# Two attention stages: weighted sums and later scores in one visit, both heads' products alternating, softmax steps half a step later

## The reference

```python
def fox_attention(q, k, v, log_f):
    ...
        s = jnp.einsum('bqhd,bkhd->bhqk', qi.astype(jnp.float32), kf) * scale
        s = s + ci[..., None] - c[:, :, None, :]
        ...
        p = jax.nn.softmax(s, axis=-1).astype(v.dtype)
        return jnp.einsum('bhqk,bkhd->bqhd', p, v)

def second_block(x, norm_g, fox_w_in, fox_b_f, fox_w_out, swa_w_in, swa_sinks, swa_w_out, final_g):
    ...
            y = fox_attention(q, k, v, log_f)          # layer 0; layer 1: swa_attention(q, k, v, sinks)
    ...
        y = y * jax.nn.silu(gate)
        x = x + y @ w_out
    return rmsnorm_2(x, final_g)
```

## Time and profile before

| | |
|---|---|
| time, median of 3 runs | 2133.93 us (2133.89 to 2136.4) |
| the profiled execution: its time | 2136.29 us |
| its span, first to last instruction | 2134.5 us |
| TensorE busy (its clock 0.999 of full speed) | 2119.7 us, 99% |
| VectorE busy | 1615.8 us, 76% |
| ScalarE busy | 1325.8 us, 62% |
| all the ACT_TABLE_LOADs | 24.4 us in 19 of them |

### The profile page before, as it was taken

One profiled execution on the slowest core, in us unless ns is written; L12 is line 12 of the kernel. 1 busy time (PEld: TensorE's weight loads), 2 busy tenths in 40 slices (PEclk: granted clock), 3 DMA queues, 4 the chain that ended last, 5 costly groups with the idle time before them and its releaser, 6 DMA issues.

```text
span 2134.5 us, 34503 instructions
## 1 busy us (share of the span) xinstructions
PE 2119.7 (99%) x13406; PEld 1852.0 (87%) x13406; DVE 1615.8 (76%) x2945; ACT 1325.8 (62%) x2601; POOL 9.7 (0%) x22
## 2 busy tenths in 40 slices
PE   9999999999999999999999999999999999999998
PEld 8888888888898888888888888888888888988887
DVE  7898766787688888656888867777686777698774
ACT  6866446775576666544666666555556655567764
POOL 0000000000000000000000000000000000000000
PEclk9999999999999999999999999999999999999999
DMA  7544434565465555555555555555555565554464
GB/s 273 168 152 135 153 112 146 188 239 195 158 196 190 193 193 196 197 191 194 195 192 195 190 196 188 206 170 195 183 181 176 166 200 192 193 163 151 148 207 138
DMA packets 107619, 389.31 MB, mean 182 GB/s; under 512 B 12304, under 2 KB 12560, under 8 KB 106688
## 3 DMA queue, kind: packets, MB, share of 16 engines
q1 hardware_dynamic: 105264, 377.31, 53.1%
q0 software_dynamic: 1904, 9.47, 1.2%
q10 hardware_dynamic: 288, 0.32, 0.0%
HBM read 384.34 MB, written 2.13 MB: 181 GB/s over the span
## 4 chain that ended last, share of the span: by engine, by line
PE 92%; DVE 4%; ACT 2%; issue 1%; DMA 0%; SPq 0%; DVEq 0%; ACTq 0%
PE main L564 85%; PE two L564 5%; DVE W L1041 1%; PE two L567 1%; DVE gt L1041 1%; ACT L1708 0%; DVE GK L1047 0%; ACT W L1709 0%; DMA RAW<-ws 0%; ACT NT L1709 0%; DVE PB L1041 0%; DVE GV L1047 0%; DVE GQ L1047 0%; PE main L611 0%; ACT PP L1709 0%
## 5 line engine op out<-in xcount | busy, mean ns | idle before, releaser
L1709 ACT ACTIVATE W<-RAW 128x512 fp32r<-128x512 f32 x1416 | 881.1, 629 | 623.8 <-PE main L564 620.5
L564 PE MATMUL main<-A,W 128*128 128x256 f32 (+1 forms) x7264 | 1256.2, 333 | 3.0 <-DVE W L1041 3.0
L1041 DVE TENSOR_TENSOR W<-RAW,W 128x512 fp32r<-128x512 f32 x1416 | 960.3, 687 | 359.8 <-ACT W L1709 351.3
L564 PEld LDWEIGHTS main<-A,W 128*128 128x128 f32 x7264 | 1096.7, 188 | 154.9 <-issue 8.5
L564 PE MATMUL main<-H,W 128*128 128x512 f32 (+1 forms) x1408 | 239.7, 333 | 0.0
L564 PEld LDWEIGHTS main<-H,W 128*128 128x128 f32 x1408 | 212.2, 188 | 27.4
L564 PE MATMUL main<-B,W 128*128 128x512 f32 (+1 forms) x1216 | 197.0, 324 | 0.0
L564 PEld LDWEIGHTS main<-B,W 128*128 128x128 f32 x1216 | 176.3, 188 | 20.2
L564 PE MATMUL main<-W,A 128*128 128x512 f32 (+1 forms) x672 | 150.2, 378 | 0.0
L564 PEld LDWEIGHTS main<-W,A 128*128 128x128 f32 x672 | 117.8, 188 | 22.1 <-DVE W L1041 0.5
L564 PE MATMUL main<-W,B 128*128 128x512 f32 x384 | 88.4, 390 | 0.0
(11 more groups left out here) (308 smaller groups left out, 1379.5 us busy)
## 6 DMA issues: line engine op xcount, KB each, us to landing
RAW<-ws SPq DMA_DIRECT2D x707, 512.0 KB, 3.3
CB<-cscr POOLq DMA_DIRECT2D x4, 1024.0 KB, 5.0
XT<-xT POOLq DMA_DIRECT2D x4, 512.0 KB, 5.8
MS<-memT POOLq DMA_DIRECT2D x4, 512.0 KB, 8.2
xs<-xT SPq DMA_DIRECT2D x7, 256.0 KB, 8.3
out<-YT SPq DMA_DIRECT2D x7, 256.0 KB, 2.6
CST<-cst SPq DMA_DIRECT2D x1, 1248.0 KB, 7.0
G<-g POOLq DMA_DIRECT2D x1, 1024.0 KB, 6.8
```

Source lines behind the costliest of these rows:

```text
L564: return e.matmul(o, l, r, start=start, stop=True, skip_group_check=True)
L1041: return e.tensor_tensor(o, a, b, op)
L1709: return e.activation(o, i, f, bias=bias, scale=scale, accum_out=accum)
```

## The change

In `weigh` the products of a pair become six of 128 columns (before: 256, 128, 256, 128), in an order in which the two heads take turns, and they are written to columns 384 to 511 of both banks instead of to columns 0 to 255 of the first. `weigh` moves to the half in which the scores of the next pair of the same buffers are multiplied: fox T+24 with a second start 24 halves after the first, swa T+22. The turn, VectorE's and ScalarE's steps move back by a half, the copies to Y by more. VectorE's first step of a pair now waits for the copy to Y of the pair before (`y_done`), and that copy waits for the later scores.

```diff
-T_FOX = [[END[f"fv{g}"] + 2 + 22 * (p // 2) for p in range(4)] for g in range(4)]
+T_FOX = [[END[f"fv{g}"] + 2 + 24 * (p // 2) for p in range(4)] for g in range(4)]
...
-            def weigh(b, v, cols, P):
-                for h in range(2):
-                    O = slice(64 * h, 64 * h + 64)
-                    mm(b[O, 0:256], v[:, 0, cols[h]], P[:, h, 0:256])
-                    z = mm(b[O, 128:256], v[:, 1, cols[h]], P[:, h, 256:384], start=False)
+            def weigh(two, v, cols, P):
+
+                for q, k in ((0, 0), (1, 0), (1, 1)):
+                    for h in range(2):
+                        O = slice(64 * h, 64 * h + 64)
+                        z = mm(two[q][O, 384:512], v[:, k, cols[h]], P[:, h, 128 * (q + k):128 * (q + k) + 128], start=k == 0)
                 return z
...
-                if 4 * g + p >= 2:
-                    w.wait_ge(y_done, 4 * g + p - 1)
                 for h in range(2):
                     P = slice(64 * h, 64 * h + 64)
                     z = scores(FQ[d][P, p, :], AK[d][P, p, :], two[h])
                 z.then_inc(fp_pe[lane], 1)
-                yield from ticks(12 + BEHIND)
+                yield from ticks(13 + BEHIND)
                 w.wait_ge(fp_ve[lane], F_VE * i + 3)
                 turn(PP[lane], two).then_inc(fp_pe[lane], 1)
-                yield from ticks(4)
+                yield from ticks(9)
                 w.wait_ge(fp_ac[lane], F_AC * i + 2)
+                if 4 * g + p >= 2:
+                    w.wait_ge(y_done, 4 * g + p - 1)
...
-                    w.wait_ge(y_done, 16 + m - 3)
+                    w.wait_ge(wp_ve[lane], W_VE * i)
+                    w.wait_ge(wp_ac[lane], W_AC * i)
...
-                yield from ticks(15)
+                yield from ticks(16)
...
-                yield from ticks(5)
+                yield from ticks(6)
                 w.wait_ge(wp_ve[lane], W_VE * i + 4)
                 w.wait_ge(wp_ac[lane], W_AC * i + 3)
...
-                yield from ticks(1 + BEHIND * lane)
+                yield from ticks(2 + BEHIND * lane)
                 w.wait_ge(fp_pe[lane], F_PE * i + 1)
+                if 4 * g + p >= 2:
+                    w.wait_ge(y_done, 4 * g + p - 1)
                 w.wait_ge(s_cb, 16 * (g + 1))
...
-                yield from ticks(1 + m % 2)
+                yield from ticks(2 + m % 2)
                 w.wait_ge(wp_pe[lane], F_PE * i + 1)
+                if m >= 4:
+                    w.wait_ge(y_done, 16 + m - 3)
                 z = tt(S[:], two[:, :, 0:384], bm(band, 2), ALU.min)
...
-                yield from ticks(5 + BEHIND * lane)
+                yield from ticks(6 + BEHIND * lane)
                 w.wait_ge(fp_ve[lane], F_VE * i + 2)
                 exps(PP[lane], mx, dn).then_inc(fp_ac[lane], 1)
...
-                yield from ticks(4)
-                w.wait_ge(fp_pe[lane], F_PE * i + 3)
-                copy(Y[:, 4 * g + p, :], two_[0][:, 0:256]).then_inc(y_done, 1)
+                yield from ticks(10)
+                w.wait_ge(fp_pe[lane], F_PE * i + (4 if i < 7 else 3))
+                copy(halfs(Y[:, 4 * g + p, :]), twos[lane][:, :, 384:512]).then_inc(y_done, 1)
...
-                yield from ticks(6 + m % 2)
+                yield from ticks(7 + m % 2)
...
-                yield from ticks(3)
-                w.wait_ge(wp_pe[lane], F_PE * i + 3)
+                yield from ticks(5)
+                w.wait_ge(wp_pe[lane], F_PE * i + (4 if m < 12 else 3))
...
-                copy(Y[:, m, :], bank[:, 0:256]).then_inc(y_done, 1)
+                copy(halfs(Y[:, m, :]), twos[m % 2][:, :, 384:512]).then_inc(y_done, 1)
```

More of the change, by code:

```diff
@@ L978, in fox @@
                 z.then_inc(fp_pe[lane], 1)
-                yield from ticks(12 + BEHIND)
+                yield from ticks(13 + BEHIND)
                 w.wait_ge(fp_ve[lane], F_VE * i + 3)
                 turn(PP[lane], two).then_inc(fp_pe[lane], 1)
-                yield from ticks(4)
+                yield from ticks(9)
                 w.wait_ge(fp_ac[lane], F_AC * i + 2)
+                if 4 * g + p >= 2:
+                    w.wait_ge(y_done, 4 * g + p - 1)
                 cols = [slice(64 * (2 * p + h), 64 * (2 * p + h) + 64) for h in range(2)]
-                weigh(two[0], AV[d], cols, PT[lane]).then_inc(fp_pe[lane], 1)
+                weigh(two, AV[d], cols, PT[lane]).then_inc(fp_pe[lane], 1)
             def swa(g, p):
@@ L1001, in swa @@
                 z.then_inc(wp_pe[lane], 1)
-                yield from ticks(15)
+                yield from ticks(16)
                 if m < 14:
                     w.wait_ge(wp_ve[(m + 2) % SWA_LANES], W_VE * ((m + 2) // SWA_LANES) + 1)
+                else:
+                    w.wait_ge(y_done, 16 + m - 1)
                 w.wait_ge(wp_ac[lane], W_AC * i + 2)
                 turn(PPw[lane], two, 2).then_inc(wp_pe[lane], 1)
-                yield from ticks(5)
+                yield from ticks(6)
                 w.wait_ge(wp_ve[lane], W_VE * i + 4)
                 w.wait_ge(wp_ac[lane], W_AC * i + 3)
+                if m >= 2:
+                    w.wait_ge(y_done, 16 + m - 1)
                 cols = [slice(64 * g, 64 * g + 64)] * 2
-                weigh(two[0], WV, cols, PTw[m % 2]).then_inc(wp_pe[lane], 1)
+                weigh(two, WV, cols, PTw[m % 2]).then_inc(wp_pe[lane], 1)
             w.wait_ge(s_warm, 1)
@@ L2023, in fox @@
                 lane, i = p % 2, 2 * g + p // 2
-                two_ = banks[4 + 2 * lane], banks[5 + 2 * lane]
                 mx, dn = (SM[:, 8 + 24 * lane + 4 * k:12 + 24 * lane + 4 * k] for k in range(2))
-                yield from ticks(5 + BEHIND * lane)
+                yield from ticks(6 + BEHIND * lane)
                 w.wait_ge(fp_ve[lane], F_VE * i + 2)
@@ L2038, in swa @@
                 lane, i = m % SWA_LANES, m // SWA_LANES
-                S, bank = PPw[lane], banks[4 + 2 * (m % 2)]
+                S = PPw[lane]
                 mx, dn, sk = (SM[:, 8 + 24 * lane + 4 * k:12 + 24 * lane + 4 * k] for k in range(3))
-                yield from ticks(6 + m % 2)
+                yield from ticks(7 + m % 2)
                 w.wait_ge(wp_ve[lane], W_VE * i + 2)
```

## The result

The changed kernel took 2144.27 us (median of 6 executions, 2143.23 to 2147.05), the kernel before 2134.59 (6 executions beside them): a ratio of 1.0044, 95% interval 1.0034 to 1.0054. By the medians it is slower by 9.7 us; the forecast was 2137.6 and the end of its range 2141.5. The profiled execution took 2145.62, its span is 2143.8. (The profiled execution of before had 3.4 us at half clock in its first 20 us, which that of after had not. Fox's first scores start 0.6 us earlier in the later one, and all that follows takes some 10 us longer.)

What follows compares the result with a forecast made beforehand. TensorE's own work was taken to bound the attentions, with one wait at fox's second gate. Joining -3.6, gate +5.8, swa +1.5 sum to +3.7: from the median 2133.93 to 2137.6 us, range 2131.0 to 2141.5.

Steps and rivals of the forecast that it cites:

- Joining and alternating: At the `weigh` visits: a joined one costs 1.46 in place of 1.73, thirteen times, plus 0.1 for three alone; gain 3.6.
- The rival without joining: At joined visits: the array's change of shape costs a return, so gain only 0.6, 2140.6; chance 0.05.
- Strict program order: Rival at `weigh`: products start strictly in program order, so alternating nearly halves 16 visits, some 2117; chance 0.01.
- the heads run side by side already: At `weigh`: both heads' first 256-column passes begin before any 128-column pass; the argument against strict program order.
- The second gate: Fox's second gate: late start and new order make TensorE wait 3.2 and 3.7, 6.9 in place of 1.1: +5.8.
- The chain of intervals: At fox's second gate: old trace intervals strung in new order put late low words 19.5 and 24.6 behind the visit.
- The rival of a ScalarE that stands again behind each load: At fox's second gate: ScalarE stands as long again behind three table loads, +3.9, 2141.5; chance 0.02.
- The other fox periods: Seven fox periods with the same late start but no table load: nothing left over, 0, bound 0.3 each.
- Swa's turns: Swa's turns wait for VectorE's minimum behind Y: 1.0 at half 39, 0.5 at half 94; +1.5, bounds 0 and 2.6.
- All else that moves lies beside main products with two halves or more to spare: Other moved steps (turns, copies to PT, Y in two pieces) cost nothing; the later Y is in time for the gates.

Runs made afterwards that it cites:

- apart: `joint` with every joined `weigh` one half earlier, so a half of main products stands before the scores: 2137.24 us, ratio 1.0009 to the kernel before.
- noalt: The changed kernel with head 0's six `weigh` passes ahead of head 1's, in place of taking turns: 2148.17 us in one execution.
- after2: The changed kernel run once more, unaltered, for a second profile: 2143.60 us in one execution.
- swalast: The changed kernel with swa's last two lone `weigh` visits a half earlier, their copies to Y two halves earlier: 2143.18 us, ratio 1.0037 to the kernel before.
- joint: The changed kernel with fox's second gate four halves later, `swalast`'s early Y, swa's turns a half later: 2133.27 us, ratio 0.9991 to the kernel before.
- fgate1: The changed kernel with fox's second gate one half later, lane 1's exponentials again before the Silu: 2138.93 us, ratio 1.0016 to the kernel before.
- fgate4: The changed kernel with fox's second gate four halves later, out of the pairs' way: 2135.84 us, ratio 1.0004 to the kernel before.
- loads2: `fgate4` with two more table loads between the two lanes' exponentials of fox's last two pairs: 2138.43 us in one execution.

## Why the forecast was wrong, point by point

**Joining and alternating, -3.6.** Right in size: 13 x 0.27 = 3.5 in the changed kernel; `apart` shows 0.23 of each 0.27 as the way out and back. The rival without joining is out. Strict program order is out in its strong form, but the reason given against it (the heads run side by side already) was too simple: `noalt` shows that the order matters.

**The second gate, +5.8.** The mechanism came as forecast. The chain of intervals held to 0.2 us, and by the starts of its products TensorE lost 3.2 and 3.6 (forecast 3.2 and 3.7). Mis-sized is what follows, which the sum put at nothing: the half clock behind the last late word, 1.5 more, which no row of before showed at a wait of 1.1. The term is about 7.3: 30.21 from visit to turn's end, where 120 main products and a turn without waits take 20.53 + 1.23, less the 1.1 lost before. The rival of a ScalarE that stands again behind each load is out: the Silu begins 1.29 behind the load ahead of it (1674.11 to 1675.40).

**The other fox periods, 0.** Right. VectorE waits for Y there, TensorE for nothing.

**Swa's turns, +1.5.** Forecast: 1.0 at the start of half 39 and 0.5 at half 94. The three waits are 0.48 at the turn behind half 39, 0.78 behind half 50 and 0.15 behind half 94. With the way back into a split turn the three visits take 1.49, 1.79 and 1.16 in place of 0.79 (the last turn of the kernel before, 2030.78 - 2029.99), 2.1 in all. Half 50 was missed, because the 2.8 behind the visit for Y was too early for most of swa: in the trace Y is there 2.9 behind one of the six joined visits and 3.9 to 5.0 behind the other five. At half 50 it is 4.95 (1934.14 to 1939.09), since the copy of a low part and two sets of four divisions stand ahead of it on ScalarE; then the last step of the rotation of the queries (AQ<-AQ,ROT) holds VectorE's minimum 0.3 longer:

```profile
1938.46 0.63 ACT L1719 ACTIVATE Y<-two 128x256 f32<-128x256 f32 x2
1938.79 0.69 DVE L1047 TENSOR_TENSOR AQ<-AQ,ROT 128x512 f32<-128x512 f32 x1
...
1939.39 0.95 DVE L1047 TENSOR_TENSOR PPw<-two,CST 128x768 f32<-128x768 f32 x1
...
1942.46 0.66 PE L567 MATMUL two<-CST,PPw 128*128 128x128 f32 x4 [0.78 <-DVE PPw L1047]
```

**"All else that moves lies beside main products with two halves or more to spare", 0.** This step failed, and with it the 0 that the sum had for swa's end. The copies of Y were held against the gates that read them, and not against the turn of the last two pairs, which since the change waits for them; and ScalarE is late just there. It cost 2.3 us without the clock (`after2`) and 3.8 with it.

The terms as measured, -3.5 + 7.3 + 2.1 + 2.3 to 3.8, make +8.2 to +9.7, where the medians differ by 9.7. The forecast's +3.7 is short by one missed wait, the clock behind the waits, and 0.6 at the turns. Shown by experiment: the gate's share, joining, taking turns (one execution), and that with the waits the loss goes. The clock's share is read from rows at either level; no run changed the clock alone. Shown in part: the last turn, since `swalast` took its wait away and got back 1.1 of 2.3; the turns' share was only tried together with the rest, in `joint`.

## What to carry to other kernels

When a wait is added in front of an instruction, look at every place that the same line of code serves, the last turn of a pipeline above all: there the branch for "no next one" has its own wait, and the engine that must release it is often busy with the work of the next stage. A chain of intervals strung from the old trace can be right to a few tenths; price also what TensorE does behind a wait, because part of that is lost to the clock. A change that saves 0.27 in thirteen places needs only two bad meetings with other work to lose three times as much, and moving that other work by a few halves gives the loss back (`joint`), though not all of the 3.5.

## What the hardware showed that was not expected

TensorE's granted clock went to half behind some waits of 2 to 3 us and not behind others: a wait of 1.98 at swa's last turn was followed by 3.4 us at 1.2 GHz, one of 2.04 at the same place in another execution of the same kernel by none. At that turn `fgate1`, `fgate4` and `loads2` too waited 2.0 and had 3.4 us at 1.2 GHz behind it; a wait of 1.91 at the gate in `fgate1` had none. The executions of the changed kernel differ with it: at a mean clock of 0.999 they took 2143.23 to 2144.72, at 0.997 2145.62, at 0.996 2147.05. At the gate a stretch at 1.2 GHz between the two waits cost nothing, because TensorE would have waited there anyway: 30.21 us with two such stretches and with one. And products of two heads in the two halves of the array overlap by their order: 1.46 when they take turns, 1.73 when six passes of one stand ahead of six of the other.
